# Windowed attention with its key tiles in mirrored pairs: two value products side by side, row sums by GpSimd, side work placed by a table

## The reference

```
q = rope(rmsnorm(h[:, :768]))      # 12 heads of 64, in 4 groups of 3
k = rope(rmsnorm(h[:, 768:1024]))  # 4 key heads; one serves a group
s_ctx = q @ k_ctx.T * scale        # 256 context keys, seen by every query
s_win = q @ k.T * scale            # latent keys with |key - query| <= 128
p = softmax([s_ctx, s_win, sink])  # the sink is one learned logit per head
o = p_ctx @ v_ctx + p_win @ v
```

## Time and profile before

| | |
|---|---|
| median of 3 runs | 3567.93 us (3563.82 to 3571.27) |
| the profiled execution: its time, its span | 3570.21 us, 3568.3 us |
| PE / DVE / ACT / POOL busy over the span | 91% / 44% / 29% / 10% |
| mean granted clock of TensorE | 0.949 |
| heads1 with its preparation | about 2270 to 2705.4 us |

### The profile page before, as it was taken

How to read it: one execution, slowest core, us unless ns; L and a number is a source line. 1 busy time by engine, 2 the same in 40 slices (tenths; PEclk the granted TensorE clock), 3 DMA queues, 4 the chain that set the end, 5 groups by cost and what they waited for, 6 DMA issues and landing times. The chain is left out here.

```text
span 3568.3 us, 37361 instructions
## 1 busy us (share of the span) xinstructions
PE 3263.1 (91%) x14194; PEld 2201.8 (62%) x14194; DVE 1573.2 (44%) x1938; ACT 1031.5 (29%) x1375; POOL 342.5 (10%) x253
## 2 busy tenths in 40 slices
PE   5697999999897999999999869688998899999997
PEld 0273333333386888888888757433435688888886
DVE  1312455444425544554554551434332455555554
ACT  1213455555513111121111220134443221221221
POOL 0000455455400000000000000100000000000000
PEclk8798899999999999999999989689998999999999
DMA  9610000000111111111111011000001111111111
GB/s 407 246 52 16 2 4 3 3 2 1 71 35 48 36 37 51 35 35 41 35 35 35 1 38 39 21 0 0 1 1 45 45 59 41 46 59 35 47 59 47
DMA packets 33641, 162.20 MB, mean 45 GB/s; under 512 B 3649, under 2 KB 6465, under 8 KB 23490
## 3 DMA queue, kind: packets, MB, share of 16 engines
q1 hardware_dynamic: 33570, 161.24, 12.4%
HBM read 157.03 MB, written 4.19 MB: 45 GB/s over the span
## 5 line engine op out<-in xcount | busy, mean ns | idle before, releaser
L604 PE MATMUL PS<-f_uh,f_Wh 128*128 128x512 f32 (+1 forms) x1760 | 483.4, 372 | 26.0 <-DVE f_ul L351 25.2
L604 PE MATMUL PS<-f_ul,f_Wh 128*128 128x512 f32 (+1 forms) x1760 | 481.4, 371 | 0.0
L604 PE MATMUL PS<-f_uh,f_Wl 128*128 128x512 f32 (+1 forms) x1760 | 481.2, 371 | 0.0
L753 DVE SCALAR_TENSOR_TENSOR X<-PS,mod,X 128x512 f32<-128x512 f32 (+1 forms) x440 | 306.1, 697 | 307.9 <-PE PS L604 307.9
L604 PEld LDWEIGHTS PS<-f_uh,f_Wh 128*128 128x128 f32 x1760 | 308.1, 188 | 89.8 <-issue 19.5
L604 PE MATMUL PS<-f_gh,f_WDh 128*128 128x512 f32 (+1 forms) x880 | 330.2, 375 | 19.5 <-DVE f_gl L739 17.2
L604 PEld LDWEIGHTS PS<-f_ul,f_Wh 128*128 128x128 f32 x1760 | 308.5, 188 | 59.2
L604 PEld LDWEIGHTS PS<-f_uh,f_Wl 128*128 128x128 f32 x1760 | 308.3, 188 | 59.0
L604 PE MATMUL PS<-f_gl,f_WDh 128*128 128x512 f32 (+1 forms) x880 | 325.1, 369 | 0.0
L604 PE MATMUL PS<-f_gh,f_WDl 128*128 128x512 f32 (+1 forms) x880 | 324.9, 369 | 0.0
L722 DVE SCALAR_TENSOR_TENSOR part<-PS,part,part 128x1023 f32<-128x1023 f32 (+1 forms) x132 | 130.0, 1013 | 328.5 <-ACT part L659 328.5
(11 more groups left out here) (250 smaller groups left out, 4227.1 us busy)
## 6 DMA issues: line engine op xcount, KB each, us to landing
mod_w<-in_mod_w SPq DMA_DIRECT2D x48, 1024.0 KB, 13.7
part<-in_w_up SPq DMA_DIRECT2D x88, 512.0 KB, 3.5
part<-in_w_down SPq DMA_DIRECT2D x22, 1024.0 KB, 5.5
part<-in_w_out SPq DMA_DIRECT2D x16, 512.0 KB, 3.5
X<-in_xT SPq DMA_DIRECT2D x4, 1280.0 KB, 9.8
X<-in_xT SPq DMA_DIRECT2D x1, 5120.0 KB, 16.3
part<-in_wqk SPq DMA_DIRECT2D x8, 512.0 KB, 3.4
out<-X SPq DMA_DIRECT2D x1, 4096.0 KB, 12.1
```

The lines of the kernel that those rows point to most:

```text
L604: mm = pe.matmul(ps(bank + c, hi - lo), w_, x_[:, lo:hi], start=f_, stop=l_)
L753: dve.scalar_tensor_tensor(out=X[:, m, lo:hi], in0=ps(DNB[r % 2], hi - lo), scalar=moda(layer, 5, m, 0 if lo < SEQ else 1), in1=X[:, m, lo ...
```

## The change

Only heads1 and the layout of the values are touched.

- *Pairs.* The 12 units of a head become 6 pairs (`pairs`): the two halves of context tile 8, those of tile 9, and latent tiles t and 7-t. Scores go round three PSUM banks, `pr` has three buffers of two units.
- *Values side by side.* The values lose their column of ones. `pv` writes queries 0 to 511 to PSUM partitions 0 to 63 and queries 512 to 1023 to partitions 64 to 127 of one bank, so the two products of a pair use different columns of TensorE. Tiles 3 and 4, which cross the middle, add two products of 128 columns.
- *Sums.* GpSimd adds the exponentials of a head into `acc` (9 additions); `spread` is two products of all ones with `acc` and two with the sink's exponential, again side by side. ScalarE's and VectorE's steps at a head's end work on 128x512 and twice 64x512 instead of 64x1024.
- *Side work by a table.* `plan` gives each step a pair and a side: side 0 stands between `qk` of the next pair and `pv`, side 1 behind `pv`. Offsets count from the first pair of the group. There are two buffers `kb`, and the heads of a group run in the order 2, 0, 1.
- The bank of the maxima's second part is now the one beside it, and the row of maxima goes to the same two banks as the scores for the maxima (before it had the banks of `spread`); so each `max` waits for the copy of the row before it.

```diff
+            pairs = [[(8, 0, 4), (8, 4, 8)], [(9, 0, 4), (9, 4, 8)]]
+            pairs += [[(t, *WIN[t]), (7 - t, *WIN[7 - t])] for t in range(4)]
...
+            def plan(G):
+
+                o = NP_ * G
+                for w, r in enumerate((-15, -13, -9, -7, -3)):
+                    at(o + r - 1, 0, "sq", G, w)
+                    at(o + r, 0, "nt", G, w)
+                    at(o + r, 1, "ro", G, w)
+                    at(o + r + 1, 0, "ca", G, w)
+                for jj, r in enumerate((-8, -2, 4)):
+                    for t_ in range(8):
+                        if o + r == -2:
+                            at(t_ // 2, t_ % 2, "max", G, jj, t_)
+                        else:
+                            at(o + r + t_ * 6 // 8, t_ % 4 == 1, "max", G, jj, t_)
+                    at(o + r + 5, 1, "mn", G, jj)
+                    at(o + r + 6, 0, "row", G, jj)
...
+                    def add(n, u):
+                        ac, p = acc[n % 2], pr[u % 3]
+                        pool.wait_ge(s["P"], 2 * NU * n + 2 * u + 2)
+                        if u == 1:
+                            at_least(pool, "bc", n - 1)
+                            pool.tensor_tensor(ac.rearrange("p (a b) -> p a b", a=2), pr[0], p, ALU.add)\
+                                .then_inc(s["ad"], 1)
+                        for c in range(2 if u > 1 else 0):
+                            _, q0, q1 = pairs[u][c]
+                            pool.wait_ge(s["ad"], NA * n + 2 * u - 3 + c)
+                            pool.tensor_tensor(ac[:, q0 * P:q1 * P], ac[:, q0 * P:q1 * P], p[:, c, 0:(q1 - q0) * P],
+                                               ALU.add).then_inc(s["ad"], 1)
...
+                        value(n, u, 0, 0, a0, min(a1, 4), False)
+                        mm = value(n, u, 1, 1, max(b0, 4), b1, False)
+                        if a1 > 4:
+                            value(n, u, 1, 0, b0, 4, True)
+                            mm = value(n, u, 0, 1, 4, a1, True)
+                        mm.then_inc(s["PV"], 1)
+
+                    def spread(n):
+
+                        at_least(pe, "out", done["nt"])
+                        pe.wait_ge(s["ad"], NA * (n + 1))
                         for c in range(2):
...
+                            pe.matmul(ps(NB, BANK, slice(64 * c, 64 * c + 64)), ones[:, 0:64],
+                                      acc[n % 2][:, c * BANK:(c + 1) * BANK], start=True, stop=False)
+                        pe.wait_ge(s["es"], n + 1)
                         for c in range(2):
...
+                            mm = pe.matmul(ps(NB, BANK, slice(64 * c, 64 * c + 64)), ones[64:65, 0:64],
+                                           es[64:65, c * BANK:(c + 1) * BANK], start=False, stop=True)
                         mm.then_inc(s["bc"], 1)
...
+                    def maximum(G, jj, qt):
+                        pe.wait_ge(s["cast"], NW * G + (3 if jj == 0 else 4 if qt < 4 else 5))
+                        at_least(pe, "mc", 24 * G + 8 * jj + qt)
+                        at_least(pe, "mr", done["row"])
...
+                    for n in range(C_HEADS):
+                        for u in range(NU):
+                            if u + 1 < NU:
+                                qk(n, u + 1)
+                            elif n + 1 < C_HEADS:
+                                qk(n + 1, 0)
+                            if u == 1 and n:
+                                spread(n - 1)
+                            side(NU * n + u, 0)
+                            pv(n, u)
+                            side(NU * n + u, 1)
...
+                    for n in range(C_HEADS):
+                        for u in range(NU):
+                            if u == 1 and n:
+                                finish(n - 1)
+                            side(NU * n + u, 0)
+                            side(NU * n + u, 1)
```

More of the change, by code:

```diff
@@ L1618, in heads1, with steps @@
+            for G in range(C_KV):
+                plan(G)
+            def steps(pair, side):
+                return slots.get((pair, side), [])
             with ExitStack() as c2:
@@ L1628, in at_least, with head, halved, in_halves @@
                         eng.wait_ge(s[name], value)
[L1630 to L1647, removed]
+                def head(n):
+                    return n // C_GROUP, JS[n % C_GROUP]
+                def halved(x, m):
+                    return x[:, 0:m // CTX, :]
+                def in_halves(x):
+                    return x.rearrange("p (a b) -> p a b", b=CTX)
                 @block.sync
@@ L1675, in _, with casts @@
+                    def casts(pair, side):
+                        for kind, *what in steps(pair, side):
+                            if kind == "ca":
+                                cast(*what)
+                    casts(UPFRONT, 0)
+                    for n in range(C_HEADS):
+                        for u in range(NU):
+                            add(n, u)
+                            casts(NU * n + u, 0)
                 @block.tensor
                 def _(pe):
-                    spreads = 0
@@ L1769, in _, with side @@
+                    def side(pair, which):
+                        for kind, *what in steps(pair, which):
+                            if kind == "nt":
+                                norms(*what)
+                            elif kind == "max":
+                                maximum(*what)
+                            elif kind == "row":
+                                rows(*what)
                     pe.wait_ge(s["tab"], 16)
                     pe.wait_ge(s["one"], 2)
-                    everywhere(step, pv, begin, lambda g, j: None)
@@ L1896, in _, with side @@
+                    def side(pair, which):
+                        for kind, *what in steps(pair, which):
+                            if kind == "sq":
+                                turn(*what)
+                            elif kind == "ro":
+                                rotated(*what)
+                            elif kind == "max":
+                                maximum(*what)
+                            elif kind == "mn":
+                                negated(*what)
                     dve.tensor_scalar(s8, sml[:, W_SINK:W_SINK + C_HEADS], 1 / C_SCALE, None, ALU.mult)\
```

464 lines of the change are left out of this document (227 added, 237 removed).

## The result

The changed kernel takes 3657.76 us (median of 4 runs, 3652.04 to 3663.5) against 3566.95 (4 runs beside it): ratio 1.0228, 95% interval 1.0198 to 1.0257. It is 2.3% slower. The forecast was 3557 with a range to 3582. The profiled execution took 3655.37 us.

What follows compares the result with a forecast made beforehand. TensorE's work, idle time and clock were taken to bound heads1. The stage went from 378.8 to 340 us, the start saved 4, giving a median of 3525; five falls added 32: 3557 us, range 3544 to 3570, 8 in 10 from 3522 to 3582.

Steps and rivals of the forecast that it cites:

- The products: TensorE's work in heads1: paired values save 32 us, spread costs 4 more, max steps 1; 287 us at full clock.
- The stage's sum to 340: First score to end of heads1: 287 work, 45 idle, 6.6 starting half clock and 1, against 378.8 us before.
- The waits: TensorE idle 45 us: ten of 2.1 behind spread, ten of 1.2 behind a row, three of 1.3 ahead of group's first row.
- GpSimd: Its new additions, 9.8 us a head, were costed at nothing, hidden by TensorE's scores and values.
- The start: Ahead of the first score: fewer casts to wait for and two max steps fewer, 4 us less (0 to 6).
- The clock: TensorE in heads1: five falls to half clock, each costing half of 12.94 us (6.5), 32 us in all.
- rival 2: Clock falls behind nearly every spread, eight times or more: 3577 us, up to 3610, slower than before; chance 0.13.
- the double waits: Ahead of a group's first row: three double stretches, 1.3 and 1.2 us with 0.6 of work between; one brings a fall.
- rival 1: The clock holds, at most two falls: 3525 to 3538, say 3530 us; layer 0 without falls counted for it; chance 0.25.

Runs made afterwards that it cites:

- E10: E1's spaced table with VectorE's order of E9 (finish behind the maximum of side 0 at pair 1): 3498.93 us, ratio 0.9797 to the kernel before.
- E9: The change with its own table; only VectorE takes the maximum of side 0 ahead of finish at pair 1: 3615.16 us.
- E11: E10 plus six unused full float32 products, one behind pairs 0 and 3 of each of the last three heads: 3508.75 us.
- E6: The change with one of the two max steps of pair 1 moved behind the next pair's scores, the one after it to pair 2's other side: 3606.06 us.
- E1: The change with another table: max steps spaced out, preparation moved and its rotations further apart: 3506.58 us, ratio 0.9805 to the kernel before.
- E7: E1 with one rotation of the second group's preparation three pairs earlier, at pair 0 of the first head: 3520.76 us.
- E5: The kernel before with value products of 128 columns in place of 65, softmax's sum left out, same order: 3580.34 us, one run.
- E2: The kernel before with value products of 64 columns in place of 65, softmax's sum left out, same order: 3645.82 us, one run.
- E3: The change with a score product between the two value products of each pair, so they cannot overlap: 3730.9 us, one run.
- E4: The change with four unused full float32 products behind pair 2 of each head but the first, 44 more: 3650.05 us, one run.

## Why the prediction was wrong

*The products* were right. A pair of values at 1.01 us, `spread` at 2.01 against 2.2. The work of the stage at full clock is best read from E10, where the same instructions nearly all run at full: 267.98 + 31.29 / 2 = 283.6 us, against 287 predicted. The pairs do save their 32 us. (The stage's sum to 340 counts 1 us for the two `max` steps a second time; it changes nothing.)

*The waits* were right in place and number: 2.05 us against 2.1 behind the six `spread`s that TensorE reached at full clock, 0.78 behind the four at half, and 1.20 against 1.2, ten times. Ahead of a group's first row it was 2.21 against 1.3, three times. Idle time was 35 us against 45; the four shorter waits are 5 of these 10.

*GpSimd* was right: no wait of TensorE for it in the stage. Where the clock is full at the end, it does show, once: 1.37 us at the last `spread` of E10. Its additions measure 1.0 us for 384 columns and 0.72 for 256, as taken.

*The start* gave 1.2 us, not 4: the first score came at 2325.44 in place of 2326.60. No more can be said, since in the traces of kernels that are the same up to there the first score comes between 2320.7 (E9) and 2329.05 (E11).

*The clock* is the step that failed, "each fall costs half of 12.94 us" with five falls. There were nine, which alone would have given 3525 + 9 x 6.5 = 3584: rival 2, which I had at 0.13. Its range ended at 3610 and did not hold the result either. The greater error is the length. I took 13.6 us for every fall, from the only three rows of their kind, where TensorE's values had 65 columns. Measured were 41, 41, 122.8, and 31.4 at the start in place of 13.1. In the sum (stage, change): busy time at half clock 307 us, so the clock costs 153.6 against the 39 that I had (6.6 and 32), 115 more; the work comes out 12 lower by this count, idle time 10 lower, the start 3 higher. 115 - 12 - 10 + 3 = 96 us, and the profiled execution lies 96 above its forecast (3655.4 against 3557 + 2.3).

That the double waits would bring one fall in three was an error of the same kind: all three did.

Two beliefs stand behind that. The first: that idle stretches which left the clock alone in the kernel before (1.72 us) would do so in the new one. They were harmless in that kernel. In the change every wait of 2.05 us at full clock brought a fall. Waits of 1.20 us brought nine in E6 and E9, and in E1 and E7 a wait of 0.40 was the last ahead of one. What makes such a wait harmful is not shown: waits of 1.72 us brought falls of 3.4 us with 128 columns too (E5).

The second: that the clock comes back by itself after 13.6 us of steady work. With 65 or 128 columns it came back after 13.1 and 12.3 us behind the first score. With 64 it took 69 us in E2, though two of E2's later stretches ended after 13.7. In the change and in E9 it stayed at half for over 119 us at 97 to 99% busy. In the traces with pairs nearly every rise comes within 6 us of the start of full 128x128 float32 products, those of the preparation or the added ones of E4. The exceptions are two rises without any, after 85.3 us in E6 and after 75.1 in E3, and those at the last `spread` (2668.6 in E1, 2744.7 in E9, 2786.9 in the change). In E3 two rotations of 256 columns (2400.9 and 2684.7) brought no rise. The last three heads prepare nothing, and a stretch at half that reaches them lasts long.

The prediction also says that layer 0 has no fall at all, and counts it for rival 1. Its attention has none behind 377 us, but TensorE never waits there for more than 0.40 us (timeline of the kernel before). So it said nothing of waits of 2 us:

```profile
924.99 0.72 PE L1223 MATMUL PS<-identb,part 128*1 128x128 bf16 x10 [0.40 <-DVE part L1421]
...
972.79 1.41 PE L452 MATMUL PS<-mix0h,out_wh 128*128 128x512 f32 x3 [12.01 <-DVE mix0l L474]
```

In the second of these waits, behind the attention, the clock did fall, at 964.1.

The Trainium skill, TensorE: Matmul & The Clock Gate, section Why this matters for your kernels, advises against idle gaps of over some 3 us. The falls behind 2.05 us in the change and behind 1.20 in E6 came well below that, so here it is no safe bound.

What was shown: that the change loses by the time at half clock (318 us in the stage), and that the order without waits over 0.4 us avoids most of it with the same work (E1, E10, several runs each). What single runs show: that the falls behind `spread` go with its waits (E6, E9); that 64 columns in place of 128 lengthen the half clock in the old order (E2 against E5); that the overlap isn't needed for it (E3); that full products end it (E4, and the rise in E7). What is open: which waits bring a fall beside which products (1.20 us did in E6 and E9 and not in the change, 1.72 in E5 and not before); why E6 and E3 rose without full products; why two of E1's six runs were slow; and how the 31 us at the start could be shortened, since E7's way brought a new wait. Layer 0's value products have 64 columns side by side as well, and there the clock held; with no wait over 0.40 us it was not put to the test.

## What to carry to other kernels

A pair of half-width products gave the work that was promised, and the kernel still lost, by the clock. So before columns are halved in a stretch that is bound by TensorE, take out the waits, the ones of a microsecond too; that alone turned 2.3% slower into 2.0% faster here. In these kernels the half clock mostly ended where full products stood, so a stretch without any, such as one at the end, is where a fall cost most (122.8 us at half). And price a fall of the clock by what TensorE runs behind it in the new kernel; how long the last one took in the old kernel says little.

## What the runs showed of the hardware

- At steady work of 97 to 100% TensorE's clock stayed at 1.2 GHz for 69 to 123 us with value products of 64 columns (E2, E9, the change), where behind the first score it rose after 12 to 13 us with 65 or 128 (the kernel before, E5). It was no fixed time: two stretches of E2 ended after 13.7 us.
- Four full float32 products of 128x128 by 512 per head, added to the change, shortened the stretches at half from 13.7 to 10.2 or 6.8 us and put two of 37.5 and 10.2 in place of the last, of 122.8 (E4).
- The same instructions of TensorE in the same order ran at either level: the last heads at half for 71.7 us in a trace of E1, and at full in that of E10.
- A lone value product of 64 columns between score products of 128 costs about 0.1 us per change of width more than one of 128 (27 us over some 290 changes, E2 against E5). In pairs side by side this is paid once for two.
- Reordering alone, with no instruction added or removed, moved the kernel by 159 us (3657.8 to 3498.9), from 1.0228 of the kernel before to 0.9797.
